# The first two weight chunks after three norms multiply x times the gain; the norm's factor and shift are applied to their product

## The reference, cut to what matters

```python
def rms_norm(x, g):
    xf = x.astype(jnp.float32)
    y = xf * lax.rsqrt(jnp.mean(xf * xf, axis=-1, keepdims=True) + NORM_EPS)
    return (y * g.astype(jnp.float32)).astype(x.dtype)
...
    for layer in range(DEPTH_2):
        shift_m, scale_m, gate_m, shift_f, scale_f, gate_f = ada_mod(c, ada_w[layer], ada_b[layer])
        h = modulate(rms_norm(x, norm_gains[layer, 0]), shift_m, scale_m)
        ...
        x = x + gate_m * y
        h = modulate(rms_norm(x, norm_gains[layer, 1]), shift_f, scale_f)
        x = x + gate_f * swiglu(h, ffn_w_gate_up[layer], ffn_w_down[layer])
```

## Time and profile before

| | us |
|---|---|
| median of 3 runs | 1141.18 (1140.57 to 1143.05) |
| profiled execution | 1138.4 |
| its span, first to last instruction | 1136.6 |
| TensorE busy | 1099.6 (97%) |
| VectorE busy | 790.4 (70%) |
| ScalarE busy | 584.1 (51%) |
| GpSimd busy | 83.2 (7%) |
| TensorE's share of the chain that ended last | 86% |

### The profile page before, as it was taken

How to read it: one execution, slowest core, us unless ns; L and a number is a source line. 1 busy time by engine, 2 the same in 40 slices (tenths; PEclk the granted TensorE clock), 3 DMA queues, 4 the chain that set the end, 5 groups by cost and what they waited for, 6 DMA issues and landing times.

```text
span 1136.6 us, 21755 instructions
## 1 busy us (share of the span) xinstructions
PE 1099.6 (97%) x8495; PEld 1058.2 (93%) x8495; DVE 790.4 (70%) x1397; ACT 584.1 (51%) x967; POOL 83.2 (7%) x79
## 2 busy tenths in 40 slices
PE   7998999999999999998999999999999999999998
PEld 6887999999999998598999999998899999999997
DVE  5757569999887986467777787885457656555543
ACT  5586547776544455544544444534365445444442
POOL 0000103434200000020000000000010110000010
PEclk7999989999999999698999999999999999999999
DMA  9531435766777643065867588354434535554450
GB/s 367 205 106 44 171 157 227 292 257 257 261 304 289 248 160 111 1 233 206 338 253 301 212 315 333 140 189 182 148 122 153 180 141 186 185 185 150 153 178 38
DMA packets 34397, 226.62 MB, mean 199 GB/s; under 512 B 3827, under 2 KB 4124, under 8 KB 12444
## 3 DMA queue, kind: packets, MB, share of 16 engines
q1 hardware_dynamic: 33884, 223.11, 52.0%
q0 software_dynamic: 448, 2.63, 0.6%
HBM read 224.66 MB, written 2.63 MB: 200 GB/s over the span
## 4 chain that ended last, share of the span: by engine, by line
PE 86%; DVE 6%; ACT 4%; DMA 2%; issue 1%; POOL 0%; SPq 0%; DVEq 0%; ACTq 0%; POOLq 0%
PE psum L1160 24%; PE psum L1162 23%; PE psum L1161 23%; PE psum L1236 2%; PE psum L1223 2%; PE psum L1226 2%; PE psum L1225 2%; DVE w_lo L1770 2%; PE psum L1255 1%; ACT w_hi L644 1%; PE psum L1267 1%; DVE arena L1801 1%; DMA raw<-in_gu 1%; PE psum L1322 1%; PE psum L1698 1%
## 5 line engine op out<-in xcount | busy, mean ns | idle before, releaser
L1770 DVE TENSOR_TENSOR w_lo<-raw,w_hi 128x1024 fp32r<-128x1024 f32 (+1 forms) x354 | 397.4, 1141 | 211.1 <-ACT w_hi L644 207.1
L644 ACT ACTIVATE w_hi<-raw 128x1024 fp32r<-128x1024 f32 (+1 forms) x354 | 339.8, 971 | 290.5 <-PE psum L1162 261.1
L1160 PE MATMUL psum<-h_hi,w_hi 128*128 128x256 f32 x1608 | 462.2, 287 | 4.6 <-DVE h_lo L1821 2.4
L1161 PE MATMUL psum<-h_lo,w_hi 128*128 128x256 f32 x1608 | 456.5, 284 | 0.0
L1162 PE MATMUL psum<-h_hi,w_lo 128*128 128x256 f32 x1608 | 456.4, 284 | 0.0
L1160 PEld LDWEIGHTS psum<-h_hi,w_hi 128*128 128x128 f32 x1608 | 310.1, 193 | 8.3 <-issue 6.0
L1161 PEld LDWEIGHTS psum<-h_lo,w_hi 128*128 128x128 f32 x1608 | 310.3, 193 | 0.3 <-issue 0.2
L1162 PEld LDWEIGHTS psum<-h_hi,w_lo 128*128 128x128 f32 x1608 | 310.0, 193 | 0.0
L1160 PE MATMUL psum<-hid_hi,w_hi 128*128 128x256 f32 x728 | 207.3, 285 | 5.1 <-ACT arena L761 2.0
L1161 PE MATMUL psum<-hid_lo,w_hi 128*128 128x256 f32 x728 | 206.7, 284 | 0.0
L1162 PE MATMUL psum<-hid_hi,w_lo 128*128 128x256 f32 x728 | 206.7, 284 | 0.0
(11 more groups left out here) (220 smaller groups left out, 984.9 us busy)
## 6 DMA issues: line engine op xcount, KB each, us to landing
arena<-in_ada SPq DMA_DIRECT2D x48, 1024.0 KB, 4.8
raw<-in_gu SPq DMA_DIRECT2D x44, 1024.0 KB, 6.3
raw<-in_ret_in SPq DMA_DIRECT2D x24, 1024.0 KB, 4.8
raw<-in_up SPq DMA_DIRECT2D x22, 1024.0 KB, 6.9
raw<-in_dn SPq DMA_DIRECT2D x32, 704.0 KB, 5.0
raw<-in_qkv SPq DMA_DIRECT2D x12, 1024.0 KB, 7.2
raw<-in_down SPq DMA_DIRECT2D x16, 704.0 KB, 6.0
raw<-in_ret_o SPq DMA_DIRECT2D x8, 1024.0 KB, 4.7
```

The lines of the kernel that those rows point to most:

```text
L644: nc.scalar.activation(w_hi[chunk % SPLIT_SLOTS][:, a:b], raw[chunk % RAW_SLOTS][:, a:b], ACT.Copy)\
L1160: nc.tensor.matmul(out, w[0], hc, start=start, stop=False, skip_group_check=True)
L1161: nc.tensor.matmul(out, w[0], lc, start=False, stop=False, skip_group_check=True)
L1770: tt(w_lo[s][:, a:b], raw[chunk % RAW_SLOTS][:, a:b], w_hi[s][:, a:b].bitcast(F32), ALU.subtract)\
```

## The change

For the three norms L0F, L1 and L1F (`DEFERRED`), the first two chunks of the next phase no longer wait for h. `square_unit` and the new `z_rest` write z, x times the gain, split into two parts, as each tile of x is finished; behind each tile of z stand two columns with the shift (`ZW` = 258 columns, `round_shift`, `shift_rest`). `start_chunk` multiplies chunks 0 and 1 by z into four PSUM banks of their own (`tra`, `att`), and `sums` and `spread` of the norm stand within chunk 0. ScalarE copies the four products out (`leave_first`), and the factor too (`rbc_copy`); GpSimd multiplies them by the factor (`settle`), and the readers (`silu_settled`, a product on VectorE, `ret_rotary`) add column 256, which is the product of the weights and the shift. Chunks from 2 on use h as before; its eight tiles are made in `norm_deferred` and `start_deferred`, with the split of chunk 2 between them, and the scaling reads the factor from SBUF. The dummy matmuls of the three norms go. GpSimd adds 5 or 6 squares and not 4. In ret_in h lies in `hid_hi` and `hid_lo`.

The pieces of the modulation move: none stands in att_o and at gu0's chunks 0, 1 and 3 now; there is one at 4, one at each odd chunk from 5, and at 18 and 20, and in dn0 also at 0 and 2. In dn0 and dn1 VectorE does the piece before the split (`lo`) of the next chunk, and not after it. The gain is computed before the phase ahead of the norm.

The diff, cut to its core:

```diff
...
 ADA_PIECES = 24
 ADA_STEPS = [("w_in", 10, lambda c: int(c in (KA, QA0))), ("up", 22, lambda c: c % 2), ("down", 16, lambda c: c % 2),
-             ("qkv", 12, lambda c: int(c < 5)), ("att_o", 4, lambda c: int(c >= 2)),
-             ("gu0", 22, lambda c: int(c % 2 or c == 0)), ("dn0", 16, lambda c: c % 2)]
+             ("qkv", 12, lambda c: int(c < 5)),
+             ("gu0", 22, lambda c: int(c >= 4 and (c % 2 or c in (4, 18, 20)))), ("dn0", 16, lambda c: int(c % 2 or c in (0, 2)))]
...
+    if norm in DEFERRED:
+        return 5 if norm == L0F else 6
...
+        RET_IN_AT = FT - DT
+        NORM[L1] = NORM[L1][:5] + (hid_hi[:, RET_IN_AT * S:], hid_lo[:, RET_IN_AT * S:])
+        Z_IN = {L0F: (hid_hi, hid_lo), L1: (h_hi, h_lo), L1F: (hid_hi, hid_lo)}
+        Z_PARTS = {L0F: ((0, DT, FT * S - DT * ZW),), L1: ((0, DT, 0),), L1F: ((0, 5, 2 * DT * S), (5, DT, 4 * S))}
+        rbc_copy = arena[:, 6144:6144 + S]
...
+            def settle(i, ph):
+                pool.wait_ge(rbc_copied, deferred_before(i) + 1)
+                for c in range(DEFERRED_CHUNKS):
+                    pool.wait_ge(first_left, 4 * deferred_before(i) + 2 * c + 2)
+                    for b in range(2):
+                        nc.gpsimd.tensor_tensor(settled_tile(c, b), settled_tile(c, b), rbc_copy, ALU.mult)\
+                            .then_inc(settled, 1)
             for i in range(len(NORM_GROUPS)):
...
                 act.wait_ge(lin_free[(ph.unit0 + unit) % 2], at(lambda u: (ph.unit0 + u) // 2 + 1))
                 w = DT // ph.units * S
                 cut = bass.ds(at(lambda u: u * w), w)
+                if norm in DEFERRED:
+                    for b in range(w // S):
+                        k = at(lambda u: u * (w // S) + b)
+                        nc.scalar.activation(z_cut(norm, k, 0), x[:, bass.ds(k * S, S)], ACT.Identity, scale=gains(norm, k))\
+                            .then_inc(z_hh, 1)
                 nc.scalar.activation(NORM[norm][1][:, cut], x[:, cut], ACT.Square).then_inc(sq_ready, w // S)
...
+            def round_shift(i, part=0):
+                act.wait_ge(gain_ready, (L0, L0F, L1, L1F).index(i) + 1)
+                nc.scalar.activation(z_shift(i, 0, part), shifts(i, part), ACT.Copy).then_inc(z_shift_hi, 1)
+            def leave_first(ph, c):
+                act.wait_ge(half_done, 2 * (ph.chunk0 + c + 1))
+                for b in range(2):
+                    nc.scalar.activation(settled_chunk(c)[:, b * ZW:(b + 1) * ZW], start_banks[c][b][:, 0:ZW], ACT.Copy)\
+                        .then_inc(first_left, 1)
+            def start_deferred(i):
+                ph = PH[AHEAD[i]]
+                root(i)
+                act.wait_ge(rbc_ready, i + 1)
+                nc.scalar.activation(rbc_copy, rbc, ACT.Copy).then_inc(rbc_copied, 1)
+                leave_first(ph, 0)
+                for k in range(DT):
+                    round_tile(i, k)
+                    if k in (2, 3):
+                        hi(ph.chunk0 + 2, ahead=k - 2)
+                leave_first(ph, 1)
             round_pair(0, PAIRS1)
...
                 hi(ph.chunk0 + c + 1)
+                if c == 0:
+                    round_shift(L0F)
                 if c >= 2:
                     square_unit(ph, L0F, c - 2)
             square_unit(ph, L0F, 2)
             hi(SPLIT_AHEAD[L0F], ahead=0)
             warm_root(L0F)
             square_unit(ph, L0F, 3)
+            hi(SPLIT_AHEAD[L0F], ahead=1)
+            start_deferred(L0F)
...
                     hi(ph.chunk0 + step.j + 1, step if step.i is not None else None, ph)
-                    if step.j >= 1:
-                        silu(step)
-                        round_hid(step, 1, ph.unit0)
-
-                steps(act, ph.n, 2, 1, step_)
+                    silu(step)
+                    round_hid(step, 1, ph.unit0)
+                def silu_settled(c):
+                    act.wait_ge(settled, 4 * deferred_before(L0F if ph.name == "gu0" else L1F) + 2 * c + 1)
+                    nc.scalar.activation(ff["g"][:, S * c:S * c + S], settled_tile(c, 0), ACT.Silu, bias=shift_sum(c, 0))\
+                        .then_inc(gelu_ready, 1)
+                silu_settled(0)
+                hi(ph.chunk0 + 3)
+                round_hid(Step(1), 1, ph.unit0)
+                silu_settled(1)
+                round_hid(Step(2), 1, ph.unit0)
+                steps(act, ph.n, 4, 1, step_)
                 silu(Step(ph.n))
...
                     if step.j >= 4 and step.j % 2 == 0:
                         square_unit(ph, norm, step.j // 2 - 2, step)
...
+            def start_chunk(ph, c, i, hooks={}):
+                whi, wlo = weights(ph.chunk0 + c, Step(c), ph)
+                cut2, blocks, half_at = ph.halves(c)[1][0] // P, 2 * DT, 0
+                order = [(b, k) for b in range(2) for k in range(DT)]
+                if c == 0:
+                    order.sort(key=lambda o: o[1])
+                for n, (b, k) in enumerate(order):
+                    if n in hooks:
+                        hooks[n]()
+                    at = b * DT + k
+                    if at >= cut2 and half_at == 0:
+                        half_at = 1
+                        second_half(ph, Step(c))
+                    if c == 0 and b == 0:
+                        pe.wait_ge(z_tiles, DT * deferred_before(i) + k + 1)
+                    cut = slice(at * P, at * P + P)
+                    ins = three(start_banks[c][b][:, 0:ZW], (whi[:, cut], wlo[:, cut]), z_cut(i, k, 0, ZW), z_cut(i, k, 1, ZW),
+                                k == 0, k == DT - 1)
+                    if at in (cut2 - 1, blocks - 1):
+                        ins.then_inc(half_done, 1)
+            def deferred_phase(name, i, sums_at, rhs=None, k0=lambda c: 0):
+                ph = PH[name]
+                pe.wait_ge(settled, 4 * deferred_before(i))
+                pe.wait_ge(z_shift_lo, z_parts_before(i) + len(Z_PARTS[i]))
+                start_chunk(ph, 0, i, {sums_at: lambda: sums(i), sums_at + 5: lambda: spread(i)})
+                start_chunk(ph, 1, i)
+                for c in (2, 3):
+                    pe.wait_ge(lin_free[(ph.unit0 + c) % 2], (ph.unit0 + c) // 2 - 1)
+                    by_feature(ph, Step(c), (h_tiles, tiles_before(i)) if c == 2 else None, rhs=rhs, k0=k0, free=False)
+            def swiglu_phase(name, i, sums_at):
+                ph = PH[name]
+                deferred_phase(name, i, sums_at)
+                steps(pe, ph.n, 4, 1, lambda s: by_feature(ph, s) if s.i is not None or s.j >= 4 else None)
...
-            norm(L0F)
-            up_phase("gu0", L0F)
+            swiglu_phase("gu0", L0F, 10)
...
-
-            norm(L1)
+            ret_rhs, ret_at = (hid_hi, hid_lo), RET_IN_AT
+            deferred_phase("ret_in", L1, 8, ret_rhs, lambda c: ret_at)
...
+                tt(z_shift(i, 1, part), shifts(i, part), z_shift(i, 0, part).bitcast(F32), ALU.subtract).then_inc(z_shift_lo, 1)
+            def z_rest(i, ph, unit, step=Step(0)):
+                at = (lambda f: f(unit)) if step.i is None else (lambda f: step.n(lambda c: f(c // 2 - 2)))
+                w = DT // ph.units
+                for b in range(w):
+                    k = at(lambda u: u * w + b)
+                    dve.wait_ge(z_hh, at(lambda u: DT * deferred_before(i) + u * w + b + 1))
+                    stt(z_cut(i, k, 1), x[:, bass.ds(k * S, S)], gains(i, k), z_cut(i, k, 0).bitcast(F32), ALU.mult, ALU.subtract)\
+                        .then_inc(z_tiles, 1)
...
+            def norm_deferred(i):
+                ph = PH[AHEAD[i]]
+                lo(SPLIT_AHEAD[i], ahead=0)
+                lo(SPLIT_AHEAD[i], ahead=1)
+                rstd(i)
+                _, _, tmp, gain_, shift, hi_, lo_ = NORM[i]
+                dve.wait_ge(rbc_copied, deferred_before(i) + 1)
+                def scale(k):
+                    cut = slice(k * S, (k + 1) * S)
+                    stt(tmp[:, cut], x[:, cut], gain_(k), rbc_copy, ALU.mult, ALU.mult).then_inc(t_ready, 1)
+                def rest_of(k):
+                    cut = slice(k * S, (k + 1) * S)
+                    dve.wait_ge(hh_ready, tiles_before(i) + k + 1)
+                    stt(lo_[:, cut], tmp[:, cut], shift(k), hi_[:, cut].bitcast(F32), ALU.add, ALU.subtract).then_inc(h_tiles, 1)
+                scale(0)
+                for k in range(DT):
+                    if k + 1 < DT:
+                        scale(k + 1)
+                    rest_of(k)
+                    if k in (2, 3):
+                        lo(ph.chunk0 + 2, ahead=k - 2)
             def residual_units(ph, layer, which):
...
-            lo(SPLIT_AHEAD[L0F], ahead=0)
+                if c >= 2:
+                    z_rest(L0F, ph, c - 2)
+            z_rest(L0F, ph, 2)
             out(Step(ph.n - 1))
-            units_done(dve, ph.unit0 + ph.units)
-            gain(L0F)
-            norm_h(L0F)
-            lo(SPLIT_AHEAD[L0F], ahead=1)
-
...
-
```

(43 more changed lines are left out.)

159 lines of the change are left out of this document (105 added, 54 removed).

## The result

| | before | changed |
|---|---|---|
| median of 4 executions, us | 1140.88 (1140.38 to 1143.05) | 1128.37 (1125.16 to 1129.09) |
| ratio, 95% interval | | 0.9881 (0.9858 to 0.9905) |
| profiled execution; its span | 1138.4; 1136.6 | 1129.09; 1127.3 |

A forecast was written before the change was run, and what follows sets the result against it. TensorE was taken as the bound, busy 1099.6 of 1136.6 us, so only its needless stretches could be won. Terms -8.35 - 0.1 - 0.85 + 4.7 = -4.6 from the median 1141.2 gave 1136.6 us, range 1130 to 1142.5.

The forecast's parts named there:

- the pieces: Moved modulation pieces delay VectorE, within its 2.6 us slack in gu0, then TensorE waits at dn0's start: 4.7 us lost.
- two more columns in 96 matmuls: The wider matmuls of chunks 0 and 1 in each phase: 1% of 11.5 us, 0.1 us, left out.
- The chain at the norms: Waits left at the three changed norms' next phases: gains of 8.35 us at gu0, 0.1 at ret_in, 0.85 at gu1.
- chunks 0 and 1 over bare: TensorE waits for the norm's factor in chunk 0: 1.9 us at gu0, 2.0 at ret_in and gu1.
- chunk 4: TensorE waits for chunk 2's bank, freed late by VectorE: 1.45 us at gu0 and gu1, 3.7 at ret_in.
- clock: Half clock on real matmuls after TensorE's waits at ret_in: 2.4 us, bounds 0 and 3.6; none counted at gu0, gu1.
- Rival 4: The clock falls in the gu phases too, once in each behind chunk 4, 1.8 us each: 1140.2 us; chance 0.10.
- rival 1: Cheaper restarts: no clock fall, GpSimd hidden, VectorE's slack swallows half of dn0's wait: 1129.5 us; chance 0.23.
- Rival 2: GpSimd holds VectorE up for each whole product ahead of chunk 2, 3.2 us a norm: 1144.3 us; chance 0.10.
- the 0.85 us of the working: TensorE's wait at chunk 2 for its weights' split, before 0.65 us was added for GpSimd, making 1.5.
- the last product at "about 650.8": VectorE's last gu0 product, 650.20 before, comes at about 650.8, ahead of dn0's piece and split; wait 2.1 us at chunk 1.
- Rival 3: Ada loads come late for four pieces at dn0's start, 1.5 us more each, 6 us: 1142.6 us; chance 0.07.

The follow-up runs named there:

- b_2112: Kernel before with h_hi and h_lo at 2112 numbers each, so buffers behind them lie 256 and 512 bytes later: 1137.47 us, ratio 1.0000.
- a_2112: Changed kernel with h_hi and h_lo at 2112 numbers each, so buffers behind them lie 256 and 512 bytes later than before: 1139.69 us, ratio 0.9993.
- b_pieces: Kernel before with only the modulation pieces moved, and in dn0 and dn1 the piece ahead of the split: 1137.42 us, ratio 0.9987.
- experiment 4: Buffer places: kernel before with the changed kernel's h_hi and h_lo sizes, 1131.50 us; with 2112 numbers each, 1137.47; changed kernel with 2112 each, 1139.69.
- b_wide: Kernel before with h_hi and h_lo 16 numbers longer each, as the changed kernel allocates them, and nothing else: 1131.50 us, ratio 0.9953.
- experiment 2: Three dummy matmuls ahead of each of the attention's first three heads' turns: kernel before 1134.57 and 1135.45 us, changed kernel 1129.21 us.
- b_shift: Kernel before with 22 more dummy matmuls ahead of qkv's first chunk, starting everything behind about 2.6 us later: 1136.63 us, ratio 0.9971.

## Why the prediction was wrong

Three things make up the 12.5 us. The schedule, which is all that the forecast is about, is worth 1 to 3 us and not 4.6, because the price of the pieces was mis-sized. The place of the buffers, which the forecast left out with "two more columns in 96 matmuls", is worth 6 to 8. The rest, 3.6 us, is luck: the mean of many executions is 8.9 us lower, not 12.5. The spread was misjudged too. The forecast took 2.3 us for what a measurement can tell, from three executions; single executions scatter by 4 us (standard deviation).

**The chain at the norms: right.** Measured against the terms, us:

| | chunks 0 and 1 over bare | chunk 2 | chunk 3 | chunk 4 | clock | sum |
|---|---|---|---|---|---|---|
| gu0, forecast | 1.9 | 1.5 | 1.6 | 1.45 | 0 | 6.45 |
| gu0, measured | 2.6 | 1.29 | 1.54 | 0.96 | 0 | 6.4 |
| ret_in, forecast | 2.0 | 1.5 | 0 | 3.7 | 2.4 | 9.6 |
| ret_in, measured | 2.6 | 1.25 | 0 | 3.75 | 1.7 | 9.3 |
| gu1, forecast | 2.0 | 1.5 | 1.6 | 1.45 | 0 | 6.55 |
| gu1, measured | 2.6 | 1.19 | 1.56 | 1.06 | 0 | 6.4 |

The first column is worked out: in gu0 516.85 - 1.29 - 501.40 = 14.16 us for two chunks, bare 11.52. Three sums come out within 0.3 us. Rival 4 (the clock falls in the gu phases) did not come, and of rival 1 nothing but 0.7 us of clock. Rival 2 is out: it needed 3.2 us at chunk 2. VectorE and GpSimd beside each other ahead of gu0, two rows of each that overlap (the row of 0.47 is VectorE's same operation alone):
```profile
510.32 1.51 POOL L663 TENSOR_TENSOR arena<-arena 128x256 f32<-128x256 f32 x2 [8.10 <-ACT arena L1096]
```
```profile
510.28 1.05 DVE L2274 SCALAR_TENSOR_TENSOR h_lo<-arena,mod,h_hi 128x256 fp32r<-128x256 f32 x1 [0.19 <-ACT h_hi L732]
511.26 0.86 DVE L2269 SCALAR_TENSOR_TENSOR arena<-x,gscale,arena 128x256 f32<-128x256 f32 x1
512.04 0.47 DVE L2274 SCALAR_TENSOR_TENSOR h_lo<-arena,mod,h_hi 128x256 fp32r<-128x256 f32 x1
```
1.51 us of GpSimd cost VectorE 0.58 + 0.39 = 0.97 us, and TensorE, if the 0.85 us of the working are right, 1.29 - 0.85 = 0.44 where I had put 0.65. The Trainium skill ("SBUF — State Buffer", "SBUF: two separate sides") says that one of the two blocks fully for a whole instruction; the trace agrees that GpSimd's products hold VectorE up, and not for the whole of their time. At chunk 4 the terms of the forecast, added up as they are written, give a wait of 1.05 us and not 1.45 (21.7 + 1.2 + 2.8 + 2.4 + 0.4 = 28.5), and 0.96 and 1.06 were measured. Chunks 0 and 1 came out 0.6 to 0.7 us dearer than forecast, and the errors hide each other in the sums.

**The pieces: mis-sized, 4.7 forecast, about 8 measured.** dn0 is 6.0 us longer (6.75 between b_2112 and a_2112), and gu0's end, which I had put inside VectorE's slack, has waits of 0.89 and 1.10 (0.42 and 0.80 in a_2112). The term that failed is the last product at "about 650.8", 0.6 us later than before: VectorE was further behind. VectorE in the changed kernel:
```profile
636.36 1.22 DVE L2000 CUSTOM_DVE_ANT_0 arena<-arena 128x1024 f32<-128x1024 f32 x1
...
638.84 0.42 DVE L2197 TENSOR_TENSOR arena<-psum,arena 128x256 f32<-128x256 f32 x1
...
640.28 1.23 DVE L2000 CUSTOM_DVE_ANT_0 arena<-arena 128x1024 f32<-128x1024 f32 x1
...
642.77 1.69 DVE L1916 TENSOR_TENSOR w_lo<-raw,w_hi 128x768 fp32r<-128x768 f32 x2
```
The piece of gu0's chunk 21 stands ahead of the last product, which so starts at 638.84, and dn0's first piece stands between that product and the split. TensorE arrived at 643.87 - 4.04 = 639.83, 1.0 us behind the start of the last product, where my terms had 653.5 - 650.8 = 2.7. These 1.7 us are most of the difference between 4.04 and 2.1. I had let VectorE fall back by 0.3 us a chunk against a slack of 2.6. A part of the error is in the sum itself: 2.4 + 0.4 + 0.5 + 0.4 + 2.5 is 6.2 and not 6.1, so 0.44 a chunk, and with the quicker pace of this execution (48 x 117.8 ns = 5.65 us a chunk) 0.55. The slack was used up a chunk before the end, where the waits of 0.89 and 1.10 lie. At chunks 2 to 4 the wait was 0.37 and not 0.95, and the clock cost 1.7 for my 1.0. Rival 3 (late ada loads) is small: VectorE waited for them twice, 1.21 and 0.52 us, in dn0. b_pieces shows the loss in a kernel that has nothing else of the change.

With this term right, the sum for the schedule is -8.35 - 0.1 - 0.85 + 8 = -1.3 us. The stages of b_2112 and a_2112, attention left out, give -1.6 (-6.21 + 6.75 - 1.26 - 0.92), and the times of experiment 4 give -1.7 with a standard error of 1.1.

**The buffers: missing.** 6 to 8 us come from the line at which I had stopped at "two more columns in 96 matmuls", 0.1 us. b_wide and a_2112 show it from both sides. In the executions about 3.7 us of it stand as time at full clock (1110.2 to 1106.4, 1110.7 to 1107.1) and the rest as less time at half clock (2.6 and 5 us in the mean, known to some 1.3 and 1.8), but by the second limit of the measure this is no division by cause. The traces give the pace directly. From start to start of back-to-back 128x256 matmuls at full clock, over all 6500 to 6900 of them, the mean is 120.16 ns in b_2112 and 119.31 in b_wide, 5.9 us in all; it is 120.08 in a_2112 and 119.05 to 119.16 in the three profiles of the changed kernel, 6.0 to 6.8 us. So the pace alone can be nearly all of it. It could not be read from the trace of before. What could be read there is the attention at half clock, in the earlier trace rows a part of TensorE's 1099.6 us busy: I took a fallen attention as fixed, though the three times shown gave no reason for it, and a fall behind gaps of 0.41 and 0.67 us stood against my own use of such gaps as proof that short waits are harmless.

**Open.** Why the clock falls in the attention in some executions and not in others, and whether moved buffers make it rarer, is not settled. The gaps are needed (experiment 2). Of the executions of kernels with displaced buffers 10 of 60 are high-loss, of those whose moving operands lie as before, without the dummies and the shift, 87 of 190. But in the profiles without dummies, which show the attention itself, it ran at half clock in 3 of 6 with displaced operands and in 4 of 8 with the others (b_shift among them). If there is an effect, whether the quicker pace has it, or only the other times at which it brings TensorE there, was not separated. What switches the quicker pace on and off within an execution is open too.

## What to carry to other kernels

Price a new buffer size too. Before a schedule is credited with a gain, run the old kernel with the new allocation, since every later buffer has moved. When a kernel's executions spread over a per cent, take a dozen of each, and read the cause from stages and from the distance between starts; the granted clock of the whole execution alone does not say where the time went. And work a steady backlog through to its last chunk: an engine that falls back 0.3 us a chunk is harmless until the one chunk at which its slack ends, and there the whole queue behind it is late at once.

## What was not expected of the hardware

- The pace of back-to-back 128x256 fp32r matmuls depends on where the moving operand begins in SBUF: 120.0 ns (502 in 60 us) with operands at the old place or 256 and 512 bytes from it, 117.8 (512) with `h_lo` moved by 64 bytes and 118.7 with hid moved by 128, and then in some stretches only. The Trainium skill ("SBUF — State Buffer", "SBUF: two separate sides") says that TensorE's port never waits on anyone; whether it is a wait there that the place changes, no run here shows.
- TensorE's clock fell behind gaps of 0.41 and 0.67 us in the attention in 7 of the 14 profiles without dummies there, and then stayed at half for 17 to 21 us; in the changed kernel it stayed at 1.00 at the gu phases' start behind 1.3, 1.5 and 1.0 us of idle time within 14 us.
